# A 128-byte pad moved from behind x's low rows to ahead of them

## What is computed

```python
def token_mixer(h, lp, pool_buf, conv_buf, ssd_state, start_pos):
    proj = jnp.einsum('bld,dk->blk', h, lp['w_in'])     # x @ w_in
    ...
    out = jnp.einsum('bld,de->ble', merged, lp['w_out'])

def decoder_layer(x, ...):
    mix, ... = token_mixer(x, ...)
    x = layer_norm(ALPHA * x + mix, ...)
    ca = memory_attention(x, ...)
    x = layer_norm(ALPHA * x + ca, ...)
    f = einsum(silu(x @ w_gate) * (x @ w_up), w_down)
    x = layer_norm(ALPHA * x + f, ...)
```

## Time and profile before

| | us |
|---|---|
| median of 3 runs | 2112.96 (2112.93 to 2114.61) |
| the profiled execution's own time | 2113.2 |
| its span, first to last instruction | 2111.6 |
| TensorE busy | 2093.1 |
| VectorE busy | 1480.2 |
| ScalarE busy | 1117.8 |
| GpSimd busy | 161.8 |

### The profile page before, as it was taken

How to read it: one execution, slowest core, us unless ns; L and a number is a source line. 1 busy time by engine, 2 the same in 40 slices (tenths; PEclk the granted TensorE clock), 3 DMA queues, 4 the chain that set the end, 5 groups by cost and what they waited for, 6 DMA issues and landing times.

```text
span 2111.6 us, 47660 instructions
## 1 busy us (share of the span) xinstructions
PE 2093.1 (99%) x17400; PEld 2076.1 (98%) x17400; DVE 1480.2 (70%) x2394; ACT 1117.8 (53%) x1671; POOL 161.8 (8%) x298
## 2 busy tenths in 40 slices
PE   9999999999999999999999999999999999999997
PEld 8999999999999999999999999999999999999997
DVE  8788877888788988444546876977666666445545
ACT  6566556566545545444434465656666665433333
POOL 1000000000002332000000010001111110000000
PEclk9999999999999999999999999999999999999998
DMA  7555555555567998555555575468888887555553
GB/s 282 198 171 185 192 185 184 164 188 185 191 194 246 309 294 269 180 179 182 176 185 203 183 287 193 164 217 291 276 292 280 281 287 255 172 188 180 180 181 110
DMA packets 125363, 451.78 MB, mean 214 GB/s; under 512 B 16057, under 2 KB 16313, under 8 KB 124233
## 3 DMA queue, kind: packets, MB, share of 16 engines
q1 hardware_dynamic: 101232, 366.41, 51.0%
q0 software_dynamic: 24048, 84.20, 12.9%
HBM read 427.87 MB, written 23.99 MB: 214 GB/s over the span
## 4 chain that ended last, share of the span: by engine, by line
PE 94%; DVE 3%; ACT 1%; DMA 1%; issue 1%; ACTq 0%; POOL 0%; DVEq 0%; SPq 0%
PE G L405 26%; PE G L406 26%; PE G L407 26%; PE M L405 4%; PE M L406 4%; PE M L407 4%; DVE sb_wlo L1401 1%; PE M L517 1%; PE M L529 1%; DMA sb_raw<-in_wstream 0%; ACT sb_whi L874 0%; DVE sb_resid L1686 0%; PE M L520 0%; PE M L500 0%; ACT sb_resid L1373 0%
## 5 line engine op out<-in xcount | busy, mean ns | idle before, releaser
L1401 DVE TENSOR_TENSOR sb_wlo<-sb_raw,sb_whi 128x1024 fp32r<-128x1024 f32 x688 | 834.5, 1223 | 563.6 <-ACT sb_whi L874 560.7
L874 ACT ACTIVATE sb_whi<-sb_raw 128x1024 fp32r<-128x1024 f32 x688 | 720.9, 1057 | 745.1 <-PE G L407 625.5
L405 PE MATMUL G<-sb_xH,sb_whi 128*128 128x264 f32 (+1 forms) x3072 | 869.2, 283 | 1.7 <-DVE sb_wlo L1401 1.2
L407 PE MATMUL G<-sb_xH,sb_wlo 128*128 128x264 f32 (+1 forms) x3072 | 866.4, 282 | 0.0
L406 PE MATMUL G<-sb_xL,sb_whi 128*128 128x264 f32 (+1 forms) x3072 | 866.1, 282 | 0.0
L405 PEld LDWEIGHTS G<-sb_xH,sb_whi 128*128 128x128 f32 x3072 | 576.2, 188 | 4.5 <-DVE sb_wlo L1401 2.0
L406 PEld LDWEIGHTS G<-sb_xL,sb_whi 128*128 128x128 f32 x3072 | 576.2, 188 | 0.0
L407 PEld LDWEIGHTS G<-sb_xH,sb_wlo 128*128 128x128 f32 x3072 | 576.0, 188 | 0.0
L406 PE MATMUL G<-sb_hL,sb_whi 128*128 128x264 f32 x704 | 200.2, 284 | 0.0
L407 PE MATMUL G<-sb_hH,sb_wlo 128*128 128x264 f32 x704 | 199.7, 284 | 0.0
L405 PE MATMUL G<-sb_hH,sb_whi 128*128 128x264 f32 x704 | 199.4, 283 | 0.0
(11 more groups left out here) (383 smaller groups left out, 2952.5 us busy)
## 6 DMA issues: line engine op xcount, KB each, us to landing
sb_raw<-in_wstream SPq DMA_DIRECT2D x688, 512.0 KB, 4.2
sb_st<-in_state_ssd POOLq DMA_DIRECT2D x32, 512.0 KB, 6.5
out_new_ssd_s<-sb_st POOLq DMA_DIRECT2D x32, 512.0 KB, 4.1
sb_tmp<-in_state_ssd POOLq DMA_DIRECT2D x34, 256.0 KB, 5.0
sb_cumbc<-scr_cum POOLq DMA_DIRECT2D x8, 1024.0 KB, 5.0
sb_resid<-in_state_ssd POOLq DMA_DIRECT2D x30, 256.0 KB, 4.4
sb_kc<-in_kc POOLq DMA_DIRECT2D x8, 512.0 KB, 7.4
sb_vc<-in_vc POOLq DMA_DIRECT2D x8, 512.0 KB, 6.1
```

The lines of the kernel that those rows point to most:

```text
L405: pe.matmul(out, w, kH, start=start, stop=False)
L407: return pe.matmul(out, wlo[:, slot, col:col + P], kH, start=False, stop=stop)
L874: act.activation(whi[:, slot, :], raw[:, slot, :], ACT.Copy).then_inc(hi_ready, 1)
L1401: dve.tensor_tensor(wlo[:, slot, :], raw[:, slot, :], whi[:, slot, :].bitcast(F32), ALU.subtract)\
```

## The change

The pad of 128 bytes behind `xL` goes, and one of 128 bytes is put between `xH` and `xL`. `xL` now starts at 128 modulo 256, and so does every row of it; `xH`, the weights, `resid` and all that follows stay at the addresses that they had. The tile `planes` over both is split into `high_rows` over `xH` and `low_rows` over `xL`, and the small arrays in the gaps are taken from these. No instruction is added, removed or moved on any engine; the operands' addresses in `xL` and in its gaps are all that differs.

```diff
         with ExitStack() as under:
-            planes = alloc(under, "planes", [P, 2 * KT, X_ROW])
+            high_rows = alloc(under, "high_rows", [P, KT, X_ROW])
+            alloc(under, "to_low_rows", [P, 32])
+            low_rows = alloc(under, "low_rows", [P, KT, X_ROW])
         xH = alloc(ctx, "xH", [P, KT, X_ROW], F32R)
+        alloc(ctx, "behind_high", [P, 32])
         xL = alloc(ctx, "xL", [P, KT, X_ROW], F32R)
-        alloc(ctx, "behind_x", [P, 32])
...
-        phs = planes[:, 0:KT, GAP:GAP + NSAMP]
+        phs = high_rows[:, :, GAP:GAP + NSAMP]
...
-        dtxc = planes[:, KT:2 * KT, GAP:GAP + 4 * XPG]
-        decc = planes[:, KT:2 * KT, GAP + 4 * XPG:GAP + 8 * XPG]
-        zsamp = planes[:, KT:2 * KT, GAP + 8 * XPG:GAP + 12 * XPG]
+        dtxc = low_rows[:, :, GAP:GAP + 4 * XPG]
+        decc = low_rows[:, :, GAP + 4 * XPG:GAP + 8 * XPG]
+        zsamp = low_rows[:, :, GAP + 8 * XPG:GAP + 12 * XPG]
```

## The result

The kernel is slower, as predicted: by 15.2 us, where the prediction had 19.0.

A forecast was written before the change was run, and what follows sets the result against it. TensorE's own pace was taken as the bound: 9,792 x matmuls at 0.12208 instead of 0.12015 us add 18.9 us, 266 columns unchanged, so 2113.2 becomes 2132.1 profiled, median 2131.9 us; range 2097 to 2146.

The forecast's parts named there:

- TensorE's pace sets the time: Whole kernel: TensorE busy 2093.1 of 2111.6 us, nothing feeds it late, so any change of pace sets the end.
- The number of matmuls touched: Matmuls on x: 9,792 with 264 columns and 768 with 266, since the whole triple's pace counts.
- The pace at 0/128: x, 264 columns, high rows at 0, low at 128: 0.12208 us instead of 0.12015, +18.9 us; chance 0.58 with surroundings.
- The 266 columns: x matmuls of 266 columns: no analogue, left at 0.1245 us, 1.7 us either way.
- y, mix and h keep their paces: Blocks on y, mix and h: paces unchanged to the fourth digit, since none of their addresses move.
- The rule that spoke against it: Notes' rule of two independent SBUF read ports: offsets could not matter, time would stay 2113.
- one test, 0/0: Check of the method: y's passing rows at offset 0 gave 0.1198 us, x measured 0.1200, within 0.0002.
- both bounds of this term: x's pace from fastest and slowest rows at any offset: 0.1185 us, 2096.8, and 0.1248 us, 2158.5.
- the faster rival: x settles at the pace of h's fastest rows, gaining 16 us, about 2097; chance 0.18.
- the slow end: Upper bound for x's pace from y's rows at 192: 0.1248 us each, +45.5 us, 2158.5.
- No change: Rival: x's low-row placement doesn't matter or the triple keeps 0.1200 us, about 2113; chance 0.14.
- Much slower: Rival: x settles as badly as y's slowest row, about 2150 to 2158 us; chance 0.10.

The follow-up runs named there:

- the run on entries: TensorE alone, six offset pairs in 20 blocks each, one matmul of another length ahead of each block: 128/128 at 120.0 ns in 7, 123.3 in 13.
- The map: TensorE alone in the layer's inner loop, all 64 pairs of high/low row offsets modulo 256 from the weights, two passes: 0/0 at 120.0 ns, 0/128 at 121.7.
- the best and the worst layer: Against the kernel before: x's rows at 224/224 with low rows of y, mix, h 112 behind, 2105.44 us; both x rows at 128, 2134.64 us.
- a gain of 6.8 us: Low rows of y, mix and h put 112 bytes behind the high ones, against the kernel before: 2108.70 us, ratio 0.9983.

## Why the prediction was right, step by step

- **TensorE's pace sets the time.** Right: 14.8 us of span, 14.9 us of busy time, waits and the other engines as before.
- **The number of matmuls touched.** 9,792 were counted, 9,694 of them follow another without a break; that is 0.2 us of the sum.
- **The pace at 0/128.** Predicted 122.08 ns from the forty passing rows of h, measured 121.77. This is the term that was mis-sized: the step is +1.62 ns instead of +1.93, and +15.7 us instead of +18.9. In the feed-forward after, 960 spacings take 116.90 us and not the 117.2 that I named.
- **The 266 columns** were left where they were, plus or minus 1.7 us: -0.3. That was luck: one long stretch gained 1.3 us and the others lost 0.9.
- **y, mix and h keep their paces.** h did to 0.01 ns; y and mix became 0.15 to 0.2 ns faster with no address moved, 0.5 us together. I had written that this would mean something else than x's offset at work. The likeliest cause is still x's offset, by way of what precedes y and mix: the run on entries shows such an effect for rows like x's, but none tests it for rows that walk.
- **The rule that spoke against it.** The measured pace goes by the offset with no other engine at work, 120.0 to 126.6 ns, and it goes by the weights' own place (11.85 against 11.52 us for the same rows). The Trainium skill, page "TensorE: Matmul & The Clock Gate", section "Step-by-step: what each phase is for", has two independent read ports and a load of the next weights that takes no SBUF read bandwidth from the running matmul. By that the offsets could not matter; for this pattern the measurement decides against it.

**Right, but by a method that doesn't hold.** I read the settled pace of a pair from rows that pass through it, and had one test, 0/0 (119.8 passing, 120.0 settled). The map gives the others. y's rows at 192 take 124.8 ns in passing; 192/192 settles at 120.0. y's rows at 224 take 120.8, and 224/224 has 120.0; y's rows at 96 take 125.5, and 96/96 gave 126.6 in one pass and 121.7 in the other. h's rows at 64/192 take 118.5 in passing; 64/192 settles at 121.4 or 120.0. The time of a passing row depends on the rows ahead of it too, so it can be above and below every pace that lasts. At the two pairs of this change it was within 0.3 ns by luck. So both bounds of this term stood on nothing: no pair with 264 columns settled below 119.9 ns in any run, so the faster rival (118.5 ns, 2097) has no pair to stand on, and the slow end was real (96/96 up to 126.6) but not for the rows that I took it from. It was misread besides: the slowest repeated row of y is not the one at 192 (0.749 us) but the one at 96, with 0.753 us in all 32 of its rows, by which that bound would have been 2165 instead of 2158.5.

**The rivals.** No change fell with 121.77 in all of x. "Much slower" didn't come at 0/128, nor in any layer that was run: the slowest, both rows at 128, has 2134.6 us, and 2144 is the estimate if all its blocks fell into the slower pace. What I named as the fragile point, two settled kinds of x at the same offsets, was the right thing to distrust.

**What stays open.** The weights take part, since their place and width change the map. But narrower weights move the slow pairs rather than removing them, and the floor near 120.0 ns for 264 columns stays with a quarter of the load. Which two reads collide, if it is a collision, and why settled paces are so often the same few numbers (120.0, 121.3, 122.2, 123.3), no run here tells.

## What to carry to other kernels

In a loop bound by streamed matmuls, as this one is, the distance modulo 256 bytes between the streamed rows and the weights is worth a few per cent of the pace (120.0 to 126.6 ns here), and 1.4% of the whole kernel between the best and the worst layer that was run. Measure a map of it once with TensorE alone, for your own row length, weight width and column count, for it holds for these only. For 264 columns and fixed rows it carried over to the whole kernel within 0.2 ns at 0/128, 0/160, 192/192 and 224/224; for 266 columns it did not always (0/160: 120.0 in the map, 121.8 in the layer). Choose a pair by two properties: a low pace, and one pace whatever precedes it. An edit elsewhere can otherwise flip a fifth of the kernel's matmuls into another pace: here a gain of 6.8 us showed up as 4.2 in the span.

## What the runs showed that I had not expected

- The same 264-column matmul triple runs anywhere from 120.0 to 126.6 ns a matmul by offsets, in blocks of 96, and steps of 4 bytes of the low row already count (0/0 120.0, 0/4 122.3, 0/16 120.3).
- More columns can be faster: 0/0 takes 119.8 ns with 256 columns and 118.7 with 260, 122.2 with 262 and 120.0 with 264 (one block of 96 each).
- Two stable paces exist for one and the same instruction stream: 120.0 and 123.3 ns at 128/128, chosen by what precedes it, and then kept, in the layer for all 960 spacings read in the feed-forward.
